# Chunk stage of a diffusion layer on one core: output stores ahead of the loads in SyncE's queue, and seven load transfers a slab in place of 19

## The reference, cut to what matters

```python
def step(s, xt):
    wt, kt, vt, kkt, at = xt[:5]
    sa = einsum('bhvk,bhk->bhv', s, -kkt)
    s = (s * wt[:, :, None, :] + sa[..., None] * (kkt * at)[:, :, None, :]
         + vt[..., None] * kt[:, :, None, :])
    return s, einsum('bhvk,bhk->bhv', s, xt[5])      # xt[5] is r
```

## Time and profile before

| | us |
|---|---|
| median of 3 runs | 4237.51 (4225.91 to 4882.52) |
| profiled execution | 4227.41 |
| its span, first to last instruction | 4225.6 |
| chunk stage within the span, about | 1240 to 2336 |
| mean granted TensorE clock | 0.936 of full speed |

### The profile page before, as it was taken

The page is one execution under the profiler, slowest core; times in us unless marked ns, Lnnn a source line. Parts: engine busy times, 40 slices in busy tenths (PEclk is TensorE's granted clock), DMA queues, the critical chain, the costliest instruction groups (busy, mean ns, idle before and its releaser), DMA issues. The chain is left out here.

```text
span 4225.6 us, 94312 instructions
## 1 busy us (share of the span) xinstructions
PE 3688.7 (87%) x39674; PEld 3082.4 (73%) x39674; DVE 2139.4 (51%) x3448; ACT 1842.5 (44%) x2997; POOL 714.9 (17%) x901
## 2 busy tenths in 40 slices
PE   7999999999977767676778779999399999999993
PEld 6777878778766667666667667778388888888883
DVE  5552543643525545454445785454554445454445
ACT  6543544533424444443445544343144444444443
POOL 1110010110102222222222133400011111111111
PEclk8999999999988888888889989999599999999997
DMA  7666565555544222323231456564466666656667
GB/s 261 196 211 201 180 222 152 178 174 156 182 129 103 76 74 72 78 71 78 67 107 38 136 181 223 175 215 145 161 210 211 216 210 218 209 209 211 221 213 288
DMA packets 450626, 702.99 MB, mean 166 GB/s; under 512 B 189400, under 2 KB 328256, under 8 KB 432720
## 3 DMA queue, kind: packets, MB, share of 16 engines
q1 hardware_dynamic: 416416, 587.26, 43.5%
q0 software_dynamic: 33840, 110.40, 8.5%
HBM read 531.97 MB, written 165.56 MB: 165 GB/s over the span
## 5 line engine op out<-in xcount | busy, mean ns | idle before, releaser
L113 PE MATMUL fro__acc<-fro__hT_hi,fro__wh 128*128 128x512 f32 (+1 forms) x1608 | 629.8, 392 | 12.6 <-DVE fro__hT_lo L2676 8.9
L114 PE MATMUL fro__acc<-fro__hT_hi,fro__wl 128*128 128x512 f32 (+1 forms) x1608 | 615.1, 383 | 0.0
L115 PE MATMUL fro__acc<-fro__hT_lo,fro__wh 128*128 128x512 f32 (+1 forms) x1608 | 614.8, 382 | 0.0
L2006 DVE TENSOR_TENSOR fin__wl<-fin__raw,fin__wh 128x4096 fp32r<-128x4096 f32 x96 | 424.7, 4424 | 317.1 <-ACT fin__wh L1950 317.1
L2682 DVE TENSOR_TENSOR fro__wl<-prj__w,fro__wh 128x1024 fp32r<-128x1024 f32 x201 | 246.3, 1225 | 586.7 <-ACT fro__wh L2419 586.5
L1950 ACT ACTIVATE fin__wh<-fin__raw 128x4096 fp32r<-128x4096 f32 x96 | 348.5, 3630 | 191.1 <-PE exp__acc L115 190.3
L113 PE MATMUL exp__acc<-fin__wh,exp__xh 128*128 128x512 f32 x1024 | 399.9, 391 | 0.7 <-DVE exp__xl L2011 0.7
L115 PE MATMUL exp__acc<-fin__wl,exp__xh 128*128 128x512 f32 x1024 | 398.5, 389 | 0.0
L114 PE MATMUL exp__acc<-fin__wh,exp__xl 128*128 128x512 f32 x1024 | 398.5, 389 | 0.0
L113 PEld LDWEIGHTS fro__acc<-fro__hT_hi,fro__wh 128*128 128x128 f32 x1608 | 305.5, 190 | 87.3 <-issue 31.5
L115 PEld LDWEIGHTS fro__acc<-fro__hT_lo,fro__wh 128*128 128x128 f32 x1608 | 305.4, 190 | 59.2
(11 more groups left out here) (467 smaller groups left out, 7617.9 us busy)
## 6 DMA issues: line engine op xcount, KB each, us to landing
fin__raw<-in_w_x SPq DMA_DIRECT2D x96, 2048.0 KB, 7.6
prj__w<-in_w_z SPq DMA_DIRECT2D x201, 512.0 KB, 4.1
s_zT<-fro__pool SPq DMA_DIRECT2D x128, 256.0 KB, 4.5
fro__wm<-in_w_mod POOLq DMA_DIRECT2D x16, 1024.0 KB, 6.2
mix__gate<-s_zT SPq DMA_DIRECT2D x64, 256.0 KB
prj__xin<-in_tokens SPq DMA_DIRECT2D x18, 512.0 KB, 5.5
rwc__bon<-s_bon SPq DMA_DIRECT2D x36, 256.0 KB
s_y<-rwc__yo SPq DMA_DIRECT2D x144, 64.0 KB, 2.1
```

The lines of the kernel that those rows point to most:

```text
L113: pe.matmul(out, sh, mh, start=first, stop=False)
L114: pe.matmul(out, sl, mh, start=False, stop=False)
L115: return pe.matmul(out, sh, ml, start=False, stop=last)
L2006: ve.tensor_tensor(wl[s][:, :, :], raw[s][:, :, :], wh[s][:, :, :], ALU.subtract).then_inc(w_lo, 1)
```

## The change

Two things change in the chunk stage. In SP's loop the two `store_rows` calls, which stood behind `load` and `store_bonus`, now stand first. And the scratch tensors are laid out so that `sg`, `bb`, `kd` of a direction are one tensor `ways` of 1536 rows, and `kkn`, `rS`, `vS` one tensor `both`; each is loaded into one SBUF tensor by three transfers of [64, 12, 128] or [64, 12, 64], and `bon` by one as before. A slab's loads are then 3 + 3 + 1 = 7 transfers of the same bytes in runs of the same length (512 bytes a row in the lower half, 256 in the upper). The semaphore that DVE's scan waits for now counts the whole of `ways`.

```diff
-        each_way, both_ways = ("sg", "bb", "kd", "bon"), ("kkn", "rS", "vS")
-        ld = [{n: sb(f"{n}{u}", [P, 4, C]) for n in each_way + both_ways} for u in range(LB)]
+        ways, both, bon = [[sb(f"{n}{u}", [P, m, 4, C]) for u in range(LB)] for n, m in (("ways", 3), ("both", 3), ("bon", 1))]
+        ld = [{n: t[u][:, m, :, :] for t, ns in ((ways, ("sg", "bb", "kd")), (both, ("kkn", "rS", "vS")), (bon, ("bon",))) for m, n in enumerate(ns)}
+              for u in range(LB)]
...
-        NLD, NSG = 16, 3
+        NLD, NSG = 4, 3
...
             def load(j):
                 u, c = j % LB, slab_at(j)
-                for n in each_way + both_ways:
-                    rows = (T[n][j % 2] if n in each_way else T[n])[:, ds(c, C)].rearrange("(q p) t -> p q t", p=P)
-                    landed = lsg[u] if n == "sg" else lds[u]
-                    if n == "bon":
-                        sp.dma_start(ld[u][n][:, :, :], rows).then_inc(landed, 16)
-                        continue
-                    sp.dma_start(ld[u][n][0:HC, :, :], rows[0:HC, :, :]).then_inc(landed, 16)
+                for t, src, landed in ((ways, T["ways"][j % 2], lsg), (both, T["both"], lds)):
+                    rows, out = src[:, ds(c, C)].rearrange("(n p) t -> p n t", p=P), t[u][:, :, :, :].rearrange("p m q t -> p (m q) t")
+                    sp.dma_start(out[0:HC, :, :], rows[0:HC, :, :]).then_inc(landed[u], 16)
                     for s in range(2):
-                        sp.dma_start(ld[u][n][HC:P, :, side(s)], rows[HC:P, :, side(1 - s)]).then_inc(landed, 16)
+                        sp.dma_start(out[HC:P, :, side(s)], rows[HC:P, :, side(1 - s)]).then_inc(landed[u], 16)
+                sp.dma_start(ld[u]["bon"], T["bon"][j % 2, :, ds(c, C)].rearrange("(q p) t -> p q t", p=P)).then_inc(lds[u], 16)
...
             for h in range(SLABS + 3):
+                if exists(h - 3):
+                    store_rows(h - 3, 1)
+                if exists(h - 2):
+                    store_rows(h - 2, 0)
                 if h + LB < SLABS:
                     for n in ("dd2", "betad", "kappad", "al", "rho", "trm", "bonm"):
                         sp.wait_ge(S[n], at(n, h))
                     load(h + LB)
                 if h < SLABS:
                     store_bonus(h)
-                if exists(h - 3):
-                    store_rows(h - 3, 1)
-                if exists(h - 2):
-                    store_rows(h - 2, 0)
```

More of the change, by code:

```diff
@@ L3360 @@
 INPUTS = ("c", "c_ctx", "b_mod", "norm_g", "ret_log_decay", "ret_gn_g", "rwkv_g2", "rwkv_ln_g", "rwkv_ln_b", "w_br_ret", "w_br_rwkv", "w_out", "w_router")
-SCRATCH = {"mod_rows": [2, MOD], "zT": [NZ * P, TOK], "sg": [2, HALF, TOK], "bb": [2, HALF, TOK], "kd": [2, HALF, TOK],
-           "bon": [2, HALF, TOK], "kkn": [HALF, TOK], "vS": [HALF, TOK], "rS": [HALF, TOK], "gT": [HALF, LAT], "y": [2, TOK, HALF], "bonus": [2, P, TOK],
+SCRATCH = {"mod_rows": [2, MOD], "zT": [NZ * P, TOK], "ways": [2, 3 * HALF, TOK], "both": [3 * HALF, TOK],
+           "bon": [2, HALF, TOK], "gT": [HALF, LAT], "y": [2, TOK, HALF], "bonus": [2, P, TOK],
            "kTr": [HALF, TOK], "qTr": [HALF, TOK], "Rb": [NT, P, RH, P], "yrT": [HALF, LAT], "mixT": [D, LAT],
@@ L3398, in build @@
         T[n] = nc.dram_tensor(f"s_{n}", shape, F32).ap()
+    for m, n in enumerate(("sg", "bb", "kd")):
+        T[n] = T["ways"][:, m * HALF:(m + 1) * HALF, :]
+    for m, n in enumerate(("kkn", "rS", "vS")):
+        T[n] = T["both"][m * HALF:(m + 1) * HALF, :]
     T["out"] = nc.dram_tensor("out", [LAT, D], F32, kind="ExternalOutput").ap()
```

## The result

The changed kernel takes 4031.5 us (median of 4 runs, 4029.0 to 4032.2), the one before 4231.7 in the runs beside it: a ratio of 0.953, 95% interval 0.951 to 0.955. The forecast was 3963 with a range of 3930 to 4010, so the direction is right and the forecast gain was a third too large: 196.4 us came off the profiled span (4225.6 to 4029.2), where 264.9 were forecast. One of the four runs of the kernel before was in a slow state (4882.5 us) and does not enter the ratio; the other three took 4225.8 to 4237.5.

The account below looks back on a forecast made before the run. The prediction took ACT's wait for yo stores, queued behind SP's load issues, to bound the chunk stage. Slabs 241.8, constants 7.9 and bonus wait 15.2 sum to 264.9 us off 4227.4, giving 3963, range 3930 to 4010.

Parts of the forecast that it names:

- The bound and the stall: Chunk stage: ACT waits for late yo stores queued behind SP's load issues, 218.5 us in 31 waits, 7.05 each.
- It does not do what it says: Rival: ACT really waits for PE's outputs, so moving stores does nothing and only the start gains: 4204 us, chance 0.02.
- slower: Rival: chunk-stage loads become the bound, 35 us a slab, 146 us more, 4373 us; chance 0.02.
- The slowest is that just the wait goes: Chunk-stage slab bounds: 23.25 us if only the stall goes, 21.59 as in two late slabs without loads.
- I keep this 0.6, as the loads stay ... I keep 0.3.: Chunk-stage slab: 0.6 us for loads in flight and 0.3 for the clock, added to 21.6, giving 22.5 us.
- With the stores in front this gains nothing more in the steady slabs.: Chunk loop: seven transfers instead of 19 shorten SP's issues from 15.7 to perhaps 4.6 us, but nobody waits for them.
- the reverse risk is a burst: Chunk loop: a slab's 1.84 MB go out in 4.6 us of issues instead of 15.7; bonus store still lands in time.
- The burst's length: Chunk loop: seven issues at 0.66 us each take 4.6 us, and a slab's bytes 7.2 us at 255 GB/s.
- The start: Start of the chunk stage: twelve fewer issues bring the constants 7.9 us forward; the bonus wait's end gains 15.2 us.
- The bonus wait: Start of the chunk stage: slab 1's bo copy no longer waits for slab 0's bo store, gaining 15.2 us.
- The stall goes and something of it is given back: Rival: load bursts compete with instruction fetching and PE's operands, or the start gains nothing: 3995 to 4030 us, chance 0.12.
- Gaps of PE marked as issue of more than 1 us a slab: Chunk-stage sign that the forecast is wrong: PE standing in issue gaps for over 1 us a slab.

Follow-up runs that it names:

- e1: The kernel before with only the two store_rows calls moved to the front of SP's loop, 19 transfers a slab kept: 4022.3 us, ratio 0.952.
- e2: The changed kernel with the two store_rows calls moved back behind the loads and the bonus store, merged transfers kept: 4037.2 us, ratio 0.954.
- e3: The changed kernel without loads inside the loop, later slabs computing on old data: 3965.9 us, ratio 0.938.
- e4: The changed kernel with seven transfers a slab ahead of the loop but 19 inside it, stores still first: 4007.1 us, ratio 0.948.
- e5: The changed kernel with its seven transfers spread over the slab, behind levels of the inverse: 3996.5 us, ratio 0.945.
- e8: The changed kernel with each slab's bytes in three transfers of 128 unbroken rows, on other data: 4037.0 us, ratio 0.955.
- e6: The changed kernel with 19 transfers a slab in the loop, three at a time behind levels of the inverse: 3987.5 us, ratio 0.944.

## Why the prediction was right in direction and wrong in size

- *The bound and the stall.* Right. The 7.05 us a slab were SP's queue; e1 and e2 each remove them (e2 all but 5.5 us in all). The clock behind the `yo` copies is 1.00, where it was 0.80. "It does not do what it says" and "slower" did not come.
- *"The slowest is that just the wait goes, 23.25 us a slab; the fastest is 21.59."* Here the first step failed. The bound took the slab to be the stall plus a rest that stays. The rest did not stay. Even in e1, with the same 19 transfers, the gaps are 2.22 us and not 1.05; what else is in the slab without the stall fell from 22.20 to 21.23, while the granted clock of the slabs rose from 0.87 to 0.99, and 23.45 comes out, above the "slowest". The stall had been a cover for late code blocks. Before has 22 full blocks, where e1 has 24, but PE, with its wait for `yo` in the same time, took 6.75 us to their ends and not 3.62, so the gap there is 0.38 us and not 0.72. Of the 1.17 us by which e1's gaps are larger, 0.63 lie later than 12 us behind `bo`, where PE used to stand in the stall (0.18 against 0.81). The other 0.54 lie in the first 12 us, where the loads are no denser than before (a share of 0.38 before and 0.37 in e1, first 7 us); why these grew is open. The lower bound failed too: two slabs without loads, at 21.55 and 21.63, stood for all, and 31 of them average 22.39. The same two slabs average 21.97 over the twelve kernels, from 21.35 to 23.12, so those two were on the short side. In after the first of them took 22.06:

```profile
2064.48 0.28 ACT L354 ACTIVATE rwc__bo<-rwc__XB 128x128 f32<-128x128 f32 x1 [0.66 <-PE rwc__XB L661]
...
2086.54 0.28 ACT L354 ACTIVATE rwc__bo<-rwc__XB 128x128 f32<-128x128 f32 x1 [0.76 <-PE rwc__XB L661]
```

- *"I keep this 0.6, as the loads stay ... I keep 0.3."* The 0.9 us that I kept for loads and clock above 21.6 measured 2.95. The loads' term measured 2.16 (after less e3), not 0.6; the remaining 0.8 is the floor's.
- *"With the stores in front this gains nothing more in the steady slabs."* This is the step that put the time outside the range. No gain is right, but the merging in the loop was priced at zero and costs 1.1 us a slab (24.55 against e1's 23.45), 34 us in all. e4, which has everything but this, takes 4007.1 us and lies inside the range, though near its end. The text named the burst and its danger ("the reverse risk is a burst"), then looked only at who waits for the loads. The one who lost was no reader of them.
- *The burst's length.* 1.84 MB in 4.6 us of issues and 7.2 us of transfer was too short: the issues took 7.6 us in the slab above, and 6.8 at the start (1240.85 to 1247.63). The window of the start shows the engines full at 226 GB/s, not 255:

```profile
1240.90:1250.00 9.10, 0.00 (x0) 0.00 (x0) 2.61 (x3) 0.99 (x2) 1.45 (x6) 0.50 1.08 226
```

- *The start.* Mechanism right, sizes a little off. The constants' wait ends 5.4 us earlier and not 7.9, because the seven issues in a row take 6.8 us and not 4.6. Size alone is not the reason: spread out in e5 the same issues take 0.57 to 0.65 us in the median. The bonus wait went, but only 13.8 of its 15.2 us came back: the stretch takes 19.0 us, where 17.6 would have been left.
- *The rivals.* "The stall goes and something of it is given back. The burst of loads competes with the fetching of instructions" is what happened, as far as fetching goes; nothing was measured of PE's operands. It was given 0.12 and priced at 23.25 a slab, 1.3 us too little, and its range, 3995 to 4030, ends just below the 4031.5. "Gaps of PE marked as issue of more than 1 us a slab" had been named as the sign of it, and the trace of before already had 1.05; asking where the longer of these 49 gaps stand in PE's stream would have told what they wait for.

In the sum: 264.9 us, less 31 x (24.55 - 22.5) = 63.6 in the slabs, less 2.5 and 1.4 at the start, less 0.8 elsewhere, is 196.6 against 196.4 measured.

## What to carry to other kernels

When a stall goes, whatever was hidden behind it shows. To price the loads, take them out of the kernel that has no stall any more, rather than reading their price beside it. Moving a needed store ahead of loads in the queue was worth all of the gain (e1's 4022.3 us are even below after's 4031.5); merging transfers pays where their issuing is waited for (the start of a stage) and costs where nobody waits and PE runs hundreds of instructions meanwhile. There, small transfers spread over the loop by waits on work that goes on anyway were the cheapest of the whole kernels: 22.89 us a slab against 24.55.

## What the hardware showed that I had not expected

- PE's instructions come in 16 KB packets, one for every 256 instructions, through the same 16 DMA engines as the loads, 5.5 a slab. In the 31 slabs of the eleven kernels without the stall no packet starts before PE has crossed into the block ahead of it, so PE has less than one block's time, some 4 us here, to get it. Every PE gap of 0.7 us or more in the 31 slabs that no semaphore explains stands at one count modulo 256, in all 12 kernels.
- With 256 and 512 byte runs the DMA engines at a full share moved 206 to 226 GB/s; with 6 KB rows (e8) 397 GB/s at a share of 0.99, the mean of the 31 slabs in the 3 us that begin 2 us behind `bo`. The faster transfer did not help PE.
- An issue of a merged load took 0.6 us at the head of a burst and when spread out (e5), and up to 1.1 in the median further on in a burst. `bon`, whose shape is unchanged, took 1.44 as the last of the seven in after and 0.61 to 0.65 in before, e1 and e5.
- Two slabs near the end, in which two 1 MB tables and other data of later stages are loaded as well, took together 6.8 us more than two average ones in after (31.39 and 24.11 us), 1.1 before, and 1.5 to 7.4 in the others. In e1, e4 and e6, with 19 transfers a slab and the stores in front, the first of the two is hardly longer (22.77 to 25.08) and the second takes 27.3 to 27.5: the cost comes a slab later.
